# The first weight tile split in halves between token blocks, and later blocks transposed inside the projection, in layer one of an encoder kernel

## The chip, the cores and the metric

The kernel runs on one core of one Trainium2 chip. The metric is the device time of one execution of the whole program in microseconds (us). All arithmetic is on 32-bit values. The engines are named as in the profile: PE is TensorE (PEld its weight loads), DVE is VectorE, ACT is ScalarE, POOL is GpSimd, SP is SyncE. SP here issues nearly all DMA transfers.

## The reference

Two request batches of 256 tokens each run through two layers of an encoder with a model width of 1024. What matters here is how each layer begins:

```
h = rms_norm(x, ln_mix[l])        # 512 tokens x 1024
z = h @ w_in[l]                   # 1024 x 3488, split into
# [c_q 384 | c_kv 256 | k_rope 32 | q_B 512 | k_B 128 | v_B 128 | g_A 1024 | g_B 1024]
x = x + (sigmoid(g_A) * (MLA(c_q, c_kv, k_rope) @ W_oA)
         + sigmoid(g_B) * (WinGQA(q_B, k_B, v_B) @ W_oB)) @ W_out
x = x + HierMoE(rms_norm(x, ln_ffn[l]))   # top group, then top-2 of 8 experts in it
```

After the second layer comes a last `rms_norm`.

## The kernel before

The two batches are treated as one list of 512 tokens, cut into four token blocks of 128 (`C = 4`, index `c`), with tokens on the partitions. Every engine has one instruction stream, written out by hand in program order, and the streams meet at semaphores (`wait_ge` and `then_inc`). There is no scheduler: an engine does its instructions strictly in the order of the code. The loop over the two layers `l` is unrolled.

**Split arithmetic.** Each projection is done as three matmuls (`mm3`, L1158): an operand is cut into a high part (a rounded copy) and a low part (the rest), and the products low x high, high x low and high x high are added up in one bank of PSUM. High parts are made by ACT (a Copy), low parts by DVE (a subtraction). For weights these are `high_part` (L621) and `low_part` (L848).

**The first normalisation.** For each block `c`, ACT squares and sums the 1024 values and takes the root (`norm_root`, L626). DVE takes the reciprocal and scales the block (`norm_chunk`, L828), which raises `h_ready`. PE transposes the block in eight 128x128 pieces, four to a bank (`norm_transposes`, L1164). ACT copies the two banks to `hT_in_high` (L653), and DVE writes `hT_in_low` (`norm_low`, L841). Both are then ready for PE as the moving or the fixed operand.

**The projection.** `w_in` is loaded in five parts. Part 0 holds the columns c_kv, k_rope and v_B, 416 columns for each of 8 slices of 128 rows: 3328 values per partition, called `in_parts[0]`, or the first weight tile. It comes by two DMAs (L403, L404). PE loops over 13 output tiles `t`. The tiles 0 to 3 are the four token blocks times part 0, each 8 slices `k` of three 128x416 matmuls, so 24 matmuls. The tiles 4 to 7 use part 1 (128x384), the tiles 8 to 12 the other parts (128x512).

**Order in layer one, before.** ACT: root of block 0, root of block 1, the high part of all of part 0 (L649), roots of blocks 2 and 3, then the high copies of all blocks. DVE: scale block 0, scale block 1, the low part of all of part 0 (L866), low part of block 0, scale block 2, low part of block 1, scale block 3, low parts of blocks 2 and 3. PE: transposes of blocks 0 and 1, then tile 0; transposes of block 2, then tile 1; transposes of block 3, then tile 2; then tile 3. PE waits for `w_in0_low` and the block's two `hT_in_low` before tile 0. In layer two, part 0 is split on POOL instead (L527 to L529), far ahead.

**What follows.** After the last token block, ACT makes the high part of part 1 and DVE its low part, for tile 4. A small matmul at the start of tile 3 gives a bias table, which goes through DVE (L874) and a DMA of POOL (L539). ACT waits for that DMA before it splits parts 2 and 3 (L673 to L675). The attention stage, the output projection, the router and the expert stage follow. Their DMAs wait for counts that PE raises (`dense_used`).

Of the kernel before, what the change touches and what calls it, by code (L numbers as in the profile page):

```python
# [10 lines left out]
ALU = mybir.AluOpType  # L11
ACT = mybir.ActivationFunctionType
AX = mybir.AxisListType

P = 128
# [4 lines left out]
C = T // P  # L20
KD = D // P
# [31 lines left out]
N_KV = N_TOK - D_CQ  # L53
# [38 lines left out]
def encoder_kernel(nc, x_prompt, x_sample, rel_bias, w_in, ln_cq, ln_ckv, w_uq, w_ukv, w_oa,  # L92
# [3 lines left out]
    with ctx:  # L96
# [255 lines left out]
        N_PARAM = 7  # L352

        IN_ORDER = {1: 0, 4: 1, 2: 2, 3: 3}
        LAST_UNITS = (0, 2, 1, 3, 4, 5, 6, 7)

        def chunk_split(j):
# [154 lines left out]
        def _(pool):  # L512
# [6 lines left out]
            for l in range(L):  # L519

                if l > 0:
                    w = in_parts[0]
                    pool.wait_ge(xs_ps, pool.snap(passes_before) * (2 * PAIRS))
                    pool.nop(nofuse=True)
                    pool.wait_ge(in_in[0], l * 32 + 32)
                    pool.nop(nofuse=True)
                    pool.tensor_copy(w.flat_high, w.flat).then_inc(w_in0_high, 1)  # L527
                    pool.wait_ge(w_in0_high, l + 1)
                    pool.tensor_tensor(w.flat_low, w.flat, w.flat_high, ALU.subtract).then_inc(w_in0_low, 1)  # L529
                    pool.drain()  # L530
                pool.wait_ge(layer_done, pool.snap(passes_before) * C + C)
# [85 lines left out]
        def _(act):  # L617
# [14 lines left out]
            def norm_copy(ns, c):  # L632
# [2 lines left out]
                act.wait_ge(hT_ps, ns * 8 + 2 * c + 1)  # L635
                act.activation(hT[:, 0:4, tok], ps, ACT.Copy).then_inc(hT_act, 1)

            act.dma_start(gain, gains[0:1, :].broadcast_to([P, D])).then_inc(gain_in, 16)
            act.wait_ge(const_in, 16)
            act.activation(spare, eps, ACT.Sqrt)  # L640
            for l in range(L):

                for c in range(C):
                    act.wait_ge(x_in[c], 16)
                    act.wait_ge(layer_done, act.snap(passes_before) * C + c + 1)
                    norm_root(c)
                    if l == 0 and c == 1:
                        act.wait_ge(in_in[0], 32)
                        act.activation(in_parts[0].flat_high, in_parts[0].flat, ACT.Copy).then_inc(w_in0_high, 1)  # L649
                for c in range(C):  # L650
                    for i in (2 * c, 2 * c + 1):
                        act.wait_ge(hT_ps, l * 16 + i + 1)
                        act.activation(hT_in[0][:, 4 * (i % 2):4 * (i % 2) + 4, c * P:(c + 1) * P],  # L653
                                       bank[i % 4][:, :].rearrange("p (k t) -> p k t", k=4), ACT.Copy).then_inc(hT_in_high, 1)
                high_part(in_parts[1], in_in[1], l * 16 + 16)

                for t in range(0, NZ, 2):
# [165 lines left out]
        def _(dve):  # L823
# [36 lines left out]
            for l in range(L):  # L860
                dve.wait_ge(gain_in, l * 32 + 16)
                for c in range(C):
                    norm_chunk(l * 2, c)
                    if l == 0 and c == 1:
                        dve.wait_ge(w_in0_high, 1)
                        dve.tensor_tensor(in_parts[0].flat_low, in_parts[0].flat, in_parts[0].flat_high, ALU.subtract).then_inc(w_in0_low, 1)  # L866
                    if c >= 1:
                        norm_low(l, c - 1)
                norm_low(l, C - 1)
                low_part(l, 0, in_parts[1])  # L870
# [278 lines left out]
        def _(pe):  # L1149
# [27 lines left out]
            pe.wait_ge(const_in, 16)  # L1177
            for l in range(L):
                norm_transposes(l * 2, 0)
                norm_transposes(l * 2, 1)  # L1180

                for t in range(NZ):
                    if t >= 4:
                        pe.wait_ge((z_act, z_dve)[t % 2], l * NZ_OUT + t // 2 - 1)
                    if t < 4:
                        if 1 <= t < 3:
                            norm_transposes(l * 2, t + 1)
                        if t == 0:
                            pe.wait_ge(w_in0_low, l + 1)
                        pe.wait_ge(hT_in_low, l * 8 + 2 * t + 2)  # L1190
                    if t == 3 and l == 0:
                        pe.wait_ge(const_bias, 48)
                        mm(bank[0][0:H, :], makings[0:BUCKETS, 0:H], makings[0:BUCKETS, 512:1024], True, True).then_inc(bias_ps, 1)
                    part = 0 if t < 4 else 1 if t < 8 else 2 if t < 10 else 3 if t < NZ_K else 4
                    if t in (4, 8, 10, NZ_K):
                        pe.wait_ge(w_low, l * SPLITS + IN_ORDER[part] + 1)
                    b = z_bank(t)
                    for k in range(KD):
                        if t < 8:
                            w = in_parts[part]  # L1200
                            tok = slice(t % 4 * P, (t % 4 + 1) * P)
                            m = mm3(b[:, 0:PARTS[part][1]], [h[:, k, tok] for h in hT_in], (w.high[:, k, :], w.low[:, k, :]), k == 0, k == KD - 1)
                        else:
                            w = in_parts[part] if t < NZ_K else k_part
                            col = slice(t % 2 * P, (t % 2 + 1) * P)
                            m = mm3(b[:, :], (w.high[:, k, col], w.low[:, k, col]), [h[:, k, :] for h in hT_in], k == 0, k == KD - 1)
                    m.then_inc(z_ps, 1)
                    if t in (3, 7, 9, 11, NZ - 1):
                        pe.drain().then_inc(dense_used, 1)
# [301 lines left out]
```

## Time and profile before

| | us |
|---|---|
| median of 3 runs | 1386.55 |
| lowest and highest | 1379.80, 1386.73 |
| the profiled execution, its own time | 1388.14 |
| its span, from the first to the last instruction | 1386.3 |
| busy in it: PE, DVE, ACT, POOL | 1248.8, 551.3, 414.5, 215.7 |
| start of the first 128x416 matmul in it | 23.14 |

The profiled execution is 1.59 us above the median of the three timed runs. 1.84 us of it lie outside the span. Times in the rows below are counted from the start of the span. A busy time of an engine in parallel with another is no cost by itself: what sets the end is the chain of waits.

### The profile page before, as it was taken

How to read it: one execution, taken by the hardware profiler on the slowest of the kernel's cores; microseconds unless marked ns; L12 is line 12 of the kernel's file. 1: busy time of each engine (PE TensorE's matmuls, PEld its weight loads, DVE VectorE, ACT ScalarE, POOL GpSimd, SP SyncE). 2: the span in 40 equal slices, each digit the busy share in tenths (PEclk: the TensorE clock that was granted, in tenths of full speed). 3: DMA queues.
4: the chain of work that ended last, by engine and by line, in shares of the span. 5: the costliest groups of instructions: out<-in, count | busy, mean ns of one | idle time of the engine just before them, and what ended most of it. 6: DMA issues, size and time to landing. Idle time of an engine off the chain costs nothing.

```text
span 1386.3 us, 15934 instructions
## 1 busy us (share of the span) xinstructions
PE 1248.8 (90%) x5822; PEld 818.4 (59%) x5822; DVE 551.3 (40%) x848; ACT 414.5 (30%) x809; POOL 215.7 (16%) x214
## 2 busy tenths in 40 slices
PE   4998879999975999999899898899999579999997
PEld 4975557777763444444388655577778434444443
DVE  3345552344242233333464455434342513333335
ACT  3425662222121212222251356422231112212223
POOL 1333540000002111110204325200000031111000
PEclk9999999999995999999999999999999779999999
DMA  9503003332056999999903120043310869999991
GB/s 279 171 16 91 1 1 107 91 91 76 31 206 266 396 415 416 416 414 417 344 2 125 28 64 1 2 150 92 91 62 16 328 257 415 415 416 416 417 412 78
DMA packets 119448, 278.44 MB, mean 201 GB/s; under 512 B 12976, under 2 KB 74928, under 8 KB 102992
## 3 DMA queue, kind: packets, MB, share of 16 engines
q1 hardware_dynamic: 111680, 259.00, 49.4%
q0 software_dynamic: 6400, 13.74, 3.0%
q10 hardware_dynamic: 1296, 4.72, 0.9%
q8 instruction: 47, 0.77, 0.2%
q14 instruction: 25, 0.20, 0.0%
HBM read 279.51 MB, written 8.40 MB: 208 GB/s over the span
## 4 chain that ended last, share of the span: by engine, by line
PE 75%; DMA 10%; DVE 6%; ACT 3%; issue 3%; DVEq 1%; ACTq 1%; SPq 1%; POOL 0%; POOLq 0%
PE bank L1156 70%; DMA arena<-w_up 5%; DMA ring<-w_up 3%; PE bank L1404 2%; PE bank L1277 2%; ACT arena L743 1%; PE bank L1173 1%; DMA x<-x_prompt 1%; DVE arena L833 1%; DVE small L973 1%; DMA arena<-token_rows,idx 1%; ACT arena L747 1%; SPq L472 0%; PE bank L1443 0%; DVE arena L968 0%
## 5 line engine op out<-in xcount | busy, mean ns | idle before, releaser
L1156 PE MATMUL bank<-arena 128*64 128x512 f32 (+5 forms) x1442 | 329.6, 517 | 34.6 <-DVEq L1115 15.0
L1156 PEld LDWEIGHTS bank<-arena 128*64 128x64 f32 (+2 forms) x1442 | 153.2, 156 | 186.3 <-issue 133.5
L1156 PE MATMUL bank<-ring,arena 128*64 128x512 f32 (+1 forms) x800 | 190.6, 607 | 7.0 <-issue 2.5
L1156 PE MATMUL bank<-y_parts,chosen 128*128 128x512 f32 x512 | 135.2, 408 | 5.5 <-DVE y_parts L1139 5.3
L1156 PEld LDWEIGHTS bank<-ring,arena 128*64 128x64 f32 (+1 forms) x800 | 64.5, 142 | 121.5 <-issue 121.5
L608 POOL MEMSET arena<- 128x1024 f32 x32 | 30.7, 959 | 657.7 <-DVEq L1125 448.0
L1094 DVE TENSOR_TENSOR x<-x,bank 128x512 f32<-128x512 f32 x128 | 87.9, 687 | 61.6 <-PE bank L1156 61.6
L1156 PEld LDWEIGHTS bank<-y_parts,chosen 128*128 128x128 f32 x512 | 92.2, 191 | 28.1 <-issue 8.7
L1156 PE MATMUL bank<-hT_gate_low,w_chunk_high 128*128 128x512 f32 x256 | 103.8, 406 | 3.5 <-issue 3.1
L1156 PE MATMUL bank<-hT_gate_high,w_chunk_low 128*128 128x512 f32 x256 | 102.0, 399 | 0.0
L1156 PE MATMUL bank<-hT_gate_high,w_chunk_high 128*128 128x512 f32 x256 | 101.8, 398 | 0.0
L1130 DVE TENSOR_TENSOR arena<-arena,bank 128x256 f32<-128x256 f32 x32 | 13.5, 421 | 220.1 <-ACT arena L801 220.1
L579 POOL TENSOR_TENSOR arena<-arena,small 128x1024 f32<-128x1024 f32 x32 | 61.3, 1917 | 135.3 <-DVE small L957 135.3
L814 ACT ACTIVATE y_parts<-bank,small 128x512 fp32r<-128x512 f32 x64 | 44.0, 688 | 127.8 <-PE bank L1156 127.8
L851 DVE TENSOR_TENSOR w_chunk_low<-ring,w_chunk_high 128x3072 fp32r<-128x3072 f32 x14 | 47.0, 3359 | 85.3 <-ACT w_chunk_high L624 85.3
L1139 DVE SCALAR_TENSOR_TENSOR y_parts<-bank,small,y_parts 128x512 fp32r<-128x512 f32 x64 | 47.9, 750 | 78.7 <-ACT y_parts L814 78.7
L801 ACT ACTIVATE arena<-bank 128x256 f32<-128x256 f32 x32 | 12.3, 385 | 209.3 <-PE bank L1156 209.3
L624 ACT ACTIVATE w_chunk_high<-ring 128x3072 fp32r<-128x3072 f32 x14 | 38.8, 2772 | 88.9 <-DMA ring<-w_in 88.7
L1156 PEld LDWEIGHTS bank<-hT_gate_low,w_chunk_high 128*128 128x128 f32 x256 | 48.7, 190 | 21.2 <-issue 10.1
L1404 PE MATMUL bank<-cst,arena 128*128 128x128 f32 x256 | 41.6, 289 | 16.1 <-DMA arena<-token_rows,idx 16.1
L1156 PEld LDWEIGHTS bank<-hT_gate_high,w_chunk_high 128*128 128x128 f32 x256 | 48.6, 190 | 12.0
L1156 PEld LDWEIGHTS bank<-hT_gate_high,w_chunk_low 128*128 128x128 f32 x256 | 48.7, 190 | 11.0
(209 smaller groups left out, 1846.0 us busy)
## 6 DMA issues: line engine op xcount, KB each, us to landing
ring<-w_gate SPq DMA_DIRECT2D x32, 1024.0 KB, 14.5
ring<-w_up SPq DMA_DIRECT2D x32, 1024.0 KB, 18.8
ring<-w_down SPq DMA_DIRECT2D x32, 1024.0 KB, 18.9
arena<-w_gate SPq DMA_DIRECT2D x32, 1024.0 KB, 15.9
arena<-w_up SPq DMA_DIRECT2D x32, 1024.0 KB, 20.1
arena<-w_down SPq DMA_DIRECT2D x32, 1024.0 KB, 19.7
ring<-w_in SPq DMA_DIRECT2D x36, 512.0 KB, 6.6
ring<-w_in SPq DMA_DIRECT2D x4, 1024.0 KB, 12.7
```

What stands on the lines that cost most here:

```text
L579: pool.tensor_tensor(p_, p_, rowinv[:, n % 2, :].unsqueeze(2).broadcast_to([P, C, S]), ALU.mult).then_inc(prob_ready, 1)
L608: pool.memset(xrows[:, r % 4, :], 0.0)
L624: act.activation(part.flat_high, part.flat, ACT.Copy).then_inc(w_high, 1)
L743: e = act.activation(soft[:, n % 2, c, :], soft[:, n % 2, c, :], ACT.Exp, bias=negmax[:, n % 2, c:c + 1], scale=1.0, accum_out=rowsum[:, n ...
L747: e = act.activation(soft[:, n % 2, c, 0:S], bank[2 * (n % 2) + i][:, b * S:(b + 1) * S], ACT.Exp, bias=negmax[:, n % 2, c:c + 1], scale=M ...
L814: act.activation(y_parts[r // 2 % 2][:, 0, n, half * 512:(half + 1) * 512], bank[4 + half][:, :], ACT.Copy, scale=w_slot[:, r:r + 1]).then ...
L851: dve.tensor_tensor(part.flat_low, part.flat, part.flat_high, ALU.subtract).then_inc(w_low, 1)
L1094: dve.tensor_tensor(part, part, bank[6 + n % 2][:, :], ALU.add).then_inc(combine_done, 1)
L1139: dve.scalar_tensor_tensor(out=y[:, 1, n, cols], in0=bank[4 + half][:, :], scalar=w_slot[:, r:r + 1], in1=y[:, 0, n, cols], op0=ALU.mult, ...
L1156: return pe.matmul(out, lhsT, rhs, start=first, stop=last)
L1277: m = pe.transpose(bank[4 + b][:, (k * 2 + i) * P:(k * 2 + i + 1) * P], soft[:, m_ % 2, 2 * b + i, k * P:(k + 1) * P], ident)
L1404: m = pe.transpose(bank[u][:, k * P:(k + 1) * P], xrows[:, r % 4, at:at + P], ident)
```

## The change

The change touches layer one only (`l == 0`), apart from a counter that starts one higher in layer two because the high and the low part of the first weight tile are now made in two steps.

- ACT takes the root of block 0, makes the two halves of the high part of the first weight tile (1664 values per partition each), copies the transposed block 0, and only then takes the roots of blocks 1, 2 and 3.
- DVE scales block 0, makes the two halves of the low part, makes the low part of block 0, and only then scales block 1.
- PE transposes block 0 and goes to tile 0. The transposes of block `t + 1` are done inside tile `t`, after its first two slices (`k == 2`, so after six matmuls), for `t` of 0, 1 and 2.

```diff
+        IN0_HALVES = slice(0, 4 * (N_KV + P)), slice(4 * (N_KV + P), KD * (N_KV + P))
...
-                    pool.wait_ge(w_in0_high, l + 1)
+                    pool.wait_ge(w_in0_high, l + 2)
...
+            def norm_high(l, c):
+
+                for i in (2 * c, 2 * c + 1):
+                    act.wait_ge(hT_ps, l * 16 + i + 1)
+                    act.activation(hT_in[0][:, 4 * (i % 2):4 * (i % 2) + 4, c * P:(c + 1) * P],
+                                   bank[i % 4][:, :].rearrange("p (k t) -> p k t", k=4), ACT.Copy).then_inc(hT_in_high, 1)
...
                     norm_root(c)
-                    if l == 0 and c == 1:
+                    if l == 0 and c == 0:
                         act.wait_ge(in_in[0], 32)
-                        act.activation(in_parts[0].flat_high, in_parts[0].flat, ACT.Copy).then_inc(w_in0_high, 1)
-                for c in range(C):
-                    for i in (2 * c, 2 * c + 1):
-                        act.wait_ge(hT_ps, l * 16 + i + 1)
-                        act.activation(hT_in[0][:, 4 * (i % 2):4 * (i % 2) + 4, c * P:(c + 1) * P],
-                                       bank[i % 4][:, :].rearrange("p (k t) -> p k t", k=4), ACT.Copy).then_inc(hT_in_high, 1)
+                        for half in IN0_HALVES:
+                            act.activation(in_parts[0].flat_high[:, half], in_parts[0].flat[:, half], ACT.Copy).then_inc(w_in0_high, 1)
+                        norm_high(0, 0)
+                for c in range(int(l == 0), C):
+                    norm_high(l, c)
...
                     norm_chunk(l * 2, c)
-                    if l == 0 and c == 1:
-                        dve.wait_ge(w_in0_high, 1)
-                        dve.tensor_tensor(in_parts[0].flat_low, in_parts[0].flat, in_parts[0].flat_high, ALU.subtract).then_inc(w_in0_low, 1)
-                    if c >= 1:
+                    if l == 0 and c == 0:
+                        for i, half in enumerate(IN0_HALVES):
+                            dve.wait_ge(w_in0_high, i + 1)
+                            dve.tensor_tensor(in_parts[0].flat_low[:, half], in_parts[0].flat[:, half], in_parts[0].flat_high[:, half],
+                                              ALU.subtract).then_inc(w_in0_low, 1)
+                        norm_low(0, 0)
+                    if c >= 1 + int(l == 0):
                         norm_low(l, c - 1)
...
                 norm_transposes(l * 2, 0)
-                norm_transposes(l * 2, 1)
+                if l > 0:
+                    norm_transposes(l * 2, 1)
...
-                        if 1 <= t < 3:
+                        if l > 0 and 1 <= t < 3:
                             norm_transposes(l * 2, t + 1)
                         if t == 0:
-                            pe.wait_ge(w_in0_low, l + 1)
+                            pe.wait_ge(w_in0_low, l + 2)
...
                     for k in range(KD):
+                        if l == 0 and t < 3 and k == 2:
+                            norm_transposes(l * 2, t + 1)
```

On DVE, at the start of layer one, the order before is this (SCALAR_TENSOR_TENSOR is the scaling of a block, 128x3328 the low part of the first weight tile, `hT_in_low` the low part of a block):

```order
L831 RECIPROCAL small<-small 128x1
L833 SCALAR_TENSOR_TENSOR arena<-x,small,lns 128x1024
L831 RECIPROCAL small<-small 128x1
L833 SCALAR_TENSOR_TENSOR arena<-x,small,lns 128x1024
L866 TENSOR_TENSOR w_in_low<-ring,w_in_high 128x3328
L845 TENSOR_TENSOR hT_in_low<-bank,hT_in_high 128x4x128 x2
L831 RECIPROCAL small<-small 128x1
L833 SCALAR_TENSOR_TENSOR arena<-x,small,lns 128x1024
```

The order on DVE in the changed kernel, at the same place:

```order
L838 RECIPROCAL small<-small 128x1
L840 SCALAR_TENSOR_TENSOR arena<-x,small,lns 128x1024
L874 TENSOR_TENSOR w_in_low<-ring,w_in_high 128x1664 x2
L852 TENSOR_TENSOR hT_in_low<-bank,hT_in_high 128x4x128 x2
L838 RECIPROCAL small<-small 128x1
L840 SCALAR_TENSOR_TENSOR arena<-x,small,lns 128x1024
L838 RECIPROCAL small<-small 128x1
L840 SCALAR_TENSOR_TENSOR arena<-x,small,lns 128x1024
```

The low parts of the weight tile and of block 0 have moved ahead of the scaling of block 1.

On PE, at the start of layer one, before (L1173 are the transposes of 128x128, the rest the first matmuls of tile 0):

```order
L1173 MATMUL bank<-cst,arena 128x128 x16
L1156 MATMUL bank<-w_in_low,hT_in_high 128x416
L1156 MATMUL bank<-w_in_high,hT_in_low 128x416
L1156 MATMUL bank<-w_in_high,hT_in_high 128x416
L1156 MATMUL bank<-w_in_low,hT_in_high 128x416
```

And in the changed kernel, where L1183 are the transposes and L1166 the matmuls:

```order
L1183 MATMUL bank<-cst,arena 128x128 x8
L1166 MATMUL bank<-w_in_low,hT_in_high 128x416
L1166 MATMUL bank<-w_in_high,hT_in_low 128x416
L1166 MATMUL bank<-w_in_high,hT_in_high 128x416
L1166 MATMUL bank<-w_in_low,hT_in_high 128x416
L1166 MATMUL bank<-w_in_high,hT_in_low 128x416
L1166 MATMUL bank<-w_in_high,hT_in_high 128x416
L1183 MATMUL bank<-cst,arena 128x128 x8
L1166 MATMUL bank<-w_in_low,hT_in_high 128x416
```

Eight of the first sixteen transposes have moved behind the sixth matmul of tile 0.

On ACT, before (ACTIVATE of 128x1024 and 128x1 are the root of a block, `w_in_high` the high part of the weight tile):

```order
L628 ACTIVATE arena,small<-x 128x1024
L630 ACTIVATE small<-small,cst 128x1
L649 ACTIVATE w_in_high<-ring 128x3328
L645 ISA
L628 ACTIVATE arena,small<-x 128x1024
```

And in the changed kernel:

```order
L629 ACTIVATE arena,small<-x 128x1024
L631 ACTIVATE small<-small,cst 128x1
L658 ACTIVATE w_in_high<-ring 128x1664 x2
L643 ACTIVATE hT_in_high<-bank 128x4x128 x2
L653 ISA
L629 ACTIVATE arena,small<-x 128x1024
```

The root ahead of the weight tile is that of block 1 before and that of block 0 now, and the copies of block 0 follow the weight tile at once.

## Rows read from the trace of the kernel before

**Rows 1.** The page's chain that ended last, shares of the span by engine.

```profile
PE 75%; DMA 10%; DVE 6%; ACT 3%; issue 3%; DVEq 1%; ACTq 1%; SPq 1%; POOL 0%; POOLq 0%
```

**Rows 2.** Chain of waits, 0 to 62 us: start us, us, what (xcount).

```profile
2.93 10.71 DMA x<-x_prompt
...
13.75 1.06 ACT arena L628
...
15.15 2.99 ACTq L629
...
18.17 3.62 DVE w_in_low L866
21.79 0.60 DVE hT_in_low L845
...
23.14 6.26 PE bank L1156 x24
29.40 0.87 PE bank L1173 x8
30.27 4.54 PE bank L1156 x24
```

**Rows 3.** The second DMA of the first weight tile: ns; first and last start us.

```profile
L404 SPq DMA_DIRECT2D ring<-w_in x1: 708/708/708, 2.2 to 2.2; - x1
...
DMA to landing us min/median/max: 10.2/10.2/10.2
```

**Rows 4.** Timeline of ACT, 0 to 130 us: start us, us, what (idle before).

```profile
18.04 1.04 ACT L628 ACTIVATE arena<-x 128x1024 f32<-128x1024 f32 x1
...
20.85 2.04 ACT L653 ACTIVATE hT_in_high<-bank 128x512 fp32r<-128x512 f32 x4
```

**Rows 5.** ACT groups by form, 0 to 60 us: xcount, busy us, mean ns, idle.

```profile
L649 ACT ACTIVATE w_in_high<-ring 128x3328 fp32r<-128x3328 f32 x1 | 3.0, 2963 | 0.0
...
L624 ACT ACTIVATE w_k_high<-ring 128x1024 fp32r<-128x1024 f32 x1 | 1.1, 1079 | 0.0
```

**Rows 6.** DVE groups by form, 0 to 60 us.

```profile
L833 DVE SCALAR_TENSOR_TENSOR arena<-x,small,lns 128x1024 f32<-128x1024 f32 x4 | 5.1, 1284 | 0.3
...
L851 DVE TENSOR_TENSOR w_k_low<-ring,w_k_high 128x1024 fp32r<-128x1024 f32 x1 | 1.2, 1203 | 0.0
```

**Rows 7.** Timeline of PE, 10 to 24 us: the first three matmuls of tile 0.

```profile
23.14 0.68 PE L1156 MATMUL bank<-w_in_low,hT_in_high 128*128 128x416 f32 x1 [4.30 <-DVE hT_in_low L845]
23.62 0.55 PE L1156 MATMUL bank<-w_in_high,hT_in_low 128*128 128x416 f32 x1
23.97 0.55 PE L1156 MATMUL bank<-w_in_high,hT_in_high 128*128 128x416 f32 x1
```

**Rows 8.** Timeline of all engines, 39 to 46.5 us, where part 1 is due.

```profile
39.06 3.36 DVE L851 TENSOR_TENSOR w_in_low<-ring,w_in_high 128x3072 fp32r<-128x3072 f32 x1 [1.86 <-ACT w_in_high L624]
...
46.16 0.41 PE L1156 MATMUL bank<-w_in_low,hT_in_high 128*128 128x384 f32 x1 [0.26 <-issue]
```

**Rows 9.** Waits of PE, 100 to 210 us: us in total, times, longest us.

```profile
PE bank L1156 <- ACTq L718: 4.9, 3, 2.2
PE bank L1277 <- POOL arena L579: 3.8, 2, 2.5
PE bank L1156 <- ACT arena L706: 3.2, 2, 1.7
```

**Rows 10.** Timeline of PE in the attention stage of layer one, two sets of transposes.

```profile
111.63 1.91 PE L1277 MATMUL bank<-cst,arena 128*128 128x128 f32 x8 [2.10 <-ACT arena L695]
...
118.54 1.04 PE L1277 MATMUL bank<-cst,arena 128*128 128x128 f32 x8
```

**Rows 11.** Busy us by stretch: PE, PEld, DVE, ACT, POOL, granted clock, DMA share, GB/s.

```profile
20.00:25.00 5.00, 1.86 (x5) 1.82 (x6) 4.92 (x7) 2.82 (x7) 0.00 (x0) 1.00 1.10 351
...
110.00:115.00 5.00, 3.37 (x12) 3.05 (x13) 0.15 (x1) 2.64 (x5) 1.90 (x1) 0.67 0.77 220
...
200.00:220.00 20.00, 15.93 (x84) 11.83 (x85) 8.70 (x11) 8.96 (x19) 4.15 (x2) 0.91 0.07 21
```

## The prediction, made before the changed kernel was run

> **What bounds the kernel now.** I read the page's chain first: three quarters of the span that set the end are PE's own work [rows 1]. So a change pays here only if it lets PE start earlier, takes instructions from it, or closes a gap in it. The change removes no matmul and no byte. What is left is the time before PE's first real matmul, and I read the chain of waits at the start for it. There the reader is to see a staircase [rows 2]: the DMA of token block 1 lands at 13.64 (2.93 + 10.71), ACT takes that block's root, ACT makes the high part of the whole first weight tile, DVE makes the low part, then the low part of block 0, and PE starts tile 0 at 23.14. From there PE runs without a gap to speak of: 24 matmuls, 8 transposes, 24 matmuls, and so on. None of the first three steps is needed by tile 0 in this order: the weight tile is held up behind block 1's root on ACT, and block 1 landed later than the weight tile did. The weight tile's second DMA was issued at 2.2 and took 10.2 us, so it lay there at 12.4 [rows 3]; ACT began on it at 15.15.
>
> **The change, part by part.**
>
> Start of the weight split. ACT's wait is now for 12.4 instead of for block 1. It begins about 0.1 us after a landing (13.64 to 13.75 in [rows 2]), so at 12.5. ACT has been idle until then, since block 0's root is long done.
>
> High halves. 3328 values cost 2963 ns and 1024 values 1079 ns [rows 5], so 0.818 ns for each further value; a half of 1664 costs 1079 + 640 x 0.818 = 1602 ns. An ACT instruction starts about 0.1 before the end of the one ahead (15.15 + 2.99 against 18.04 in [rows 2, 4]). First half 12.5 to 14.1, second 14.0 to 15.6. The two copies of block 0 follow, four cost 2.04 [rows 4], so they end at about 16.6. The transposes that they read are long done: they need block 0 alone, which is first in every stream.
>
> Low halves. 3.62 us for 3328 values [rows 2] and 1203 ns for 1024 [rows 6]: 1.05 ns per value, a half costs 1203 + 640 x 1.05 = 1875 ns. DVE begins at 14.15 and ends the first half at 16.0, and the second at 17.8, DVE now being the longer of the two and ACT ahead of it. The split in halves buys the overlap: one piece of 2963 ns and then one of 3.62 us take 6.6 us, the halves 17.8 - 12.5 = 5.3.
>
> PE's start. Before, 21.79 is the end of the weight tile's low part, and PE starts 1.35 later, at 23.14, after two low parts of block 0 [rows 2]. The same step now gives 17.8 + 1.35 = 19.15. PE starts tile 0 by 23.14 - 19.15 = 4.0 us earlier. Of this some 2.7 come from the order and 1.3 from the halves.
>
> The transposes of block 1. Before, they stood in PE's wait and cost nothing; now they are in PE's stream. A set of 8 costs 0.87 in the chain [rows 2], at full clock. The sets of blocks 2 and 3 stood in the stream already, between tiles, and move inside them at the same price. Net: 4.0 - 0.87 = 3.1 us.
>
> Is what they wait for there? DVE scales block 1 only after 19.0: a reciprocal of 0.2 and 1.28 [rows 6] give 20.6. ACT has its root by then: copies end at 16.6 and two roots take 20.85 - 18.04 [rows 4], one 1.4, so 18.0, and those of blocks 2 and 3 are done at 19.4 and 20.8. PE comes to block 1 after six matmuls, 0.35 apart in this stretch [rows 7], at 19.15 + 2.2 = 21.4. Nothing is waited for, by 0.8. The price if that cover goes: were these matmuls at full clock, 4.54 / 24 = 0.19 apart [rows 2], PE would come at 20.3 and wait 0.3. Tile 1 wants block 1's low part. Transposes end near 23, ACT and DVE need 1.3 us behind them, and tile 0 still has 18 matmuls, 3.4 us: hidden. Tiles 2 and 3 have 18 matmuls of cover in the same way, where before they had 24, and the two late steps on ACT and DVE fit in either.
>
> What is next late. ACT starts the high part of weight part 1 only after the copies of block 3, whose transposes now stand 6 matmuls (1.1 us) further into tile 2. The step moves by 3.1 - 1.1 = 2.0 us and PE by 3.1. Its low part ended at 39.06 + 3.36 = 42.4 with the first 128x384 matmul at 46.16 [rows 8]: 3.7 us of slack become 2.6. The bias table, for whose DMA ACT waits before it splits parts 2 and 3, goes through DVE behind that low part and so comes some 2 us earlier; parts 2 and 3 are used by tiles 8 to 11 only, with four tiles of part 1 ahead of them. The transfers after that wait for counts of PE and move with it. POOL's wait in layer two has another number and the same event. I take these at nothing, and at most 0.3 us if I misjudge one.
>
> The sum: 1388.14 (the profiled execution, span 1386.3 and 1.84 around it) - 3.1 = 1385.0. That execution was 1.6 above the median of the runs shown; against the median it is 1386.55 - 3.1 = 1383.4. It is 0.22% of the time.
>
> **The term I can't read: the clock.** The stretch 20 to 25 shows a granted clock of 1.00 [rows 11], but the matmuls in it start 0.35 apart [rows 7] and in tile 1 0.19 [rows 2]: PE began at the 1.2 GHz level and went to 2.4 GHz about 3 us into tile 0. Tile 0 took 6.26 where tile 1 took 4.54 [rows 2], so the slow start costs 1.7 us. After the change PE does half as many transposes ahead and then has one unbroken run. If the rise comes as long after the start as before, nothing changes and 3.1 stands. If it stays at the same moment, near 26.2, then 4.0 more us run at half speed: 4.0 x 0.19 / 0.35 = 2.2 of work, less 0.87, and the gain is 1.3. If there is no slow stretch at all, the gain is 3.1 + 1.7 = 4.8. I take 3.1, since in the trace PE had also stood idle for 4.3 us before tile 0 and rose 3 us after.
>
> The Trainium skill ("TensorE: Matmul & The Clock Gate", Part 1) says that the monitor's window runs freely and isn't reset when a kernel starts, so the moment of the rise depends on how the first matmul falls in it. By that rule the rise is tied neither to the start nor to one moment, and the gain would lie anywhere between the 1.3 and the 4.8. The trace, with one start in it, doesn't tell.
>
> **The rivals.**
>
> The rise stays where it was. For it: the idle stretch before tile 0, 4.30 us [rows 7], grows, since the second set of transposes no longer stands ahead of it. Against: the rise came 3 us into the first unbroken run, as if started by it. 1386.55 - 1.3 = 1385.3.
>
> Clock drops further on fall away. The granted clock is 0.67 over 110 to 115 us, after PE waited 2.10 us for ACT; the transposes there took 1.91, and a later set 1.04 [rows 10, 11]. Such a stretch costs (1 - 0.67) x 5 = 1.65 us. Not every wait of this length has one: between 100 and 210 us there are seven others, of up to 2.5 us [rows 9], and the clock fell once more, 0.91 over 200 to 220 [rows 11]. So it hangs on timing, which a shift by 3 us alters. Two fewer, or one and an early rise at the start: 1386.55 - 3.1 - 3.3 = 1380.1. The lowest run before, 1379.80, shows that such times occur.
>
> The same mechanism the other way, and this is the case that ends slower: the waits of the attention stages, in both layers, meet the clock worse. Place: PE behind ACT L718, L706 and POOL L579. Price: 1.65 us a drop. It decides from the second additional drop (3.3 against 3.1), and with three it is +5.0 - 3.1 = +1.9: 1388.4. For it: at least six waits there drew none yet. Against: nothing in the change favours this side, and it needs three of them.
>
> The change doesn't do what it says: the start isn't freed, because the weight tile isn't the late input. If ACT got it only with block 1 at 13.64, all would move by 1.2 and the gain would be 1.9, 1384.6; if also the scaling of block 1 were late inside tile 0, where PE would stand, near 1386. Against: the landing in [rows 3] is 1.2 ahead of block 1's.
>
> **How the numbers follow.** Forecast 0.62 (1383.4, alone 1381.5 to 1385); rise stays 0.12 (1385.3); fewer drops 0.14 (1380.1); more drops 0.08 (1388.4); not freed 0.04 (1386). A measurement of this kernel can tell about 0.5%, 6.9 us, from no change, so faster by that means 1379.6 or less. Half and a little more of the fewer-drops case, makes 0.10, since a time below 1380 turned up before the change too. Slower by that is over 1393.5, which needs six drops: 0.03. The rest, 0.87, is within. The range reaches from the fewer-drops case, 1379, to the more-drops case, 1388.
>
> **What would show it.** In the profile after: the ACT instruction of 128x1664 starts near 12.5 and the last low half ends near 17.8; the first 128x416 matmul starts near 19.2; block 1's transposes begin near 21.4 with no wait for DVE; tile 1's first matmul 3 us earlier than 30.27; the first 128x384 matmul near 43.1, with no wait for the low part of part 1; and the same 3 us at every later landmark up to the attention stage. The spacing of the first matmuls shows the rise. The forecast is wrong if PE waits inside tile 0, if the 3 us are there at 43 and gone by the end with no clock drop to account for them, or if the first low half waits for its high half longer than 0.1.

## The result, and the profile after

| | before | changed |
|---|---|---|
| median of 18 runs each, us | 1385.31 | 1376.68 |
| lowest and highest | 1374.79, 1389.43 | 1371.73, 1382.52 |
| profiled execution, own time | 1388.14 | 1372.49 |

The ratio of the comparison is 0.995, with a 95% interval of 0.9932 to 0.9969: faster, by 4 to 9 us (the two medians alone give 0.9938, the two means 7.1 ± 2.6 us). The forecast was 1383.4, in a range of 1379 to 1388, so the median came out below the range. The two profiled executions lie 15.6 us apart, more than the medians do.

**The start is as the prediction had it.** The chain of waits of the changed kernel, 0 to 120 us (start us, us, what), answers to [rows 2]:

```profile
2.17 10.07 DMA ring<-w_in
12.27 1.60 ACT w_in_high L658
13.89 3.69 DVE w_in_low L874 x2
17.59 0.60 DVE hT_in_low L852
...
18.93 2.42 PE bank L1166 x6
21.35 1.50 PE bank L1183 x8
22.86 4.55 PE bank L1166 x24
27.41 0.87 PE bank L1183 x8
```

The staircase now begins with the weight tile's own DMA instead of token block 1's. The first 128x416 matmul stands at 18.93 instead of 23.14, 4.2 us earlier. PE goes from its sixth matmul to block 1's transposes without a wait. The next landmark [rows 8] moved by 3.13 us:

```profile
43.03 0.41 PE L1166 MATMUL bank<-w_in_low,hT_in_high 128*128 128x384 f32 x1 [0.26 <-issue]
```

The low part of part 1 ended at 37.05 + 3.36 = 40.4, with 2.6 us of slack, as the prediction had it:

```profile
37.05 3.36 DVE L858 TENSOR_TENSOR w_in_low<-ring,w_in_high 128x3072 fp32r<-128x3072 f32 x1 [1.86 <-ACT w_in_high L625]
```

**Where the rest comes from.** SP's issues of DMAs come in the same order in both kernels and make good landmarks: the start of such an issue says how far the program has come. Before less changed, in the first pair of traces (us from the start of the span):

| landmark | before | changed | difference |
|---|---|---|---|
| layer one, w_uq | 46.02 | 42.90 | 3.12 |
| w_oa, the first chunk | 109.77 | 106.64 | 3.13 |
| w_out, end of attention | 217.25 | 211.23 | 6.02 |
| layer two, w_in | 672.46 | 666.49 | 5.97 |
| w_uq | 728.48 | 715.61 | 12.87 |
| w_out | 899.57 | 883.79 | 15.78 |
| y_prompt | 1379.05 | 1363.43 | 15.62 |

3.1 us come from the start, 2.9 from the attention stage of layer one, 6.9 from the first steps of layer two, 2.9 from its attention stage. The change has edited no instruction in any of the last three.

The largest piece first. These are DVE and POOL of the kernel before in layer two (start us, us, what): POOL's subtraction for the first weight tile, and the last of 32 instructions of DVE that build `chosen`.

```profile
683.70 7.22 POOL L529 TENSOR_TENSOR w_in_low<-ring,w_in_high 128x3328 fp32r<-128x3328 f32 x1
683.98 7.48 DVE L1133 TENSOR_TENSOR chosen<-cst,small 128x512 fp32r<-128x512 f32 x1
```

And in the changed kernel:

```profile
678.01 0.68 DVE L1143 TENSOR_TENSOR chosen<-cst,small 128x512 fp32r<-128x512 f32 x1
678.11 7.81 POOL L530 TENSOR_TENSOR w_in_low<-ring,w_in_high 128x3328 fp32r<-128x3328 f32 x1
```

Both instructions read two operands from SBUF, the on-chip memory. The one that starts second waits for the first: with POOL 0.28 us ahead, DVE took 7.48 us instead of 0.68; with DVE 0.10 us ahead, POOL took 7.81 instead of 7.22. The Trainium skill ("SBUF — State Buffer", section "Who interferes with whom") says just this: a DVE instruction with two SBUF inputs contends with a GpSimd instruction that reads SBUF, and issue order decides who blocks. The trace agrees, and it was to be read before the run: the waits of PE in the kernel before (us in total, times, longest) had a row for it.

```profile
PE bank L1156 <- DVE y_parts L1139: 5.3, 1, 5.3
```

The changed kernel has no such row. PE also came out of this wait at the slower of its two levels: the granted clock is 0.50 from 692 to 695.

The attention stage. A drop here is a stretch in which the granted clock falls. It is the third figure from the end of a row. The first stretch of the kernel before is 110 to 115 in [rows 11], at 0.67; this is one near the end of the stage:

```profile
205.00:210.00 5.00, 3.01 (x12) 2.72 (x13) 3.08 (x3) 2.78 (x6) 1.93 (x1) 0.73 0.02 5
```

And of the changed kernel at the same two places:

```profile
107.00:112.00 5.00, 3.48 (x18) 2.84 (x19) 0.66 (x3) 2.55 (x5) 1.89 (x1) 1.00 0.76 198
195.00:200.00 5.00, 3.56 (x16) 1.66 (x16) 4.92 (x8) 3.19 (x12) 2.02 (x2) 0.66 0.00 0
```

The drop behind the wait for ACT L695 is gone; that wait itself is the same, 2.1 us in both. The second drop comes some 5 us earlier in the stage. There PE is slow while POOL is still busy with the softmax, and the next wait shrinks from 2.50 us for POOL [rows 9] to 1.29:

```profile
202.59 1.06 PE L1290 MATMUL bank<-cst,arena 128*128 128x128 f32 x8 [1.29 <-ACTq L725]
```

In this pair the drop in one place cost more than the drop in the other. What each is worth follows below, from all the traces.

### The profile page after: what moved, and what is told of

Read it like the earlier page. It is cut to its first block, busy times and chain, and to the rows that moved or that the text cites. A ratio compares the mean times of both kernels' runs of the same rounds, so it can differ in the third digit from the quotient of the medians.

```text
span 1370.7 us, 15936 instructions
## 1 busy us (share of the span) xinstructions
PE 1243.4 (91%) x5822; PEld 813.1 (59%) x5822; DVE 545.1 (40%) x849; ACT 414.5 (30%) x810; POOL 216.0 (16%) x214
## 4 chain that ended last, share of the span: by engine, by line
PE 76%; DMA 10%; DVE 5%; ACT 4%; issue 2%; DVEq 1%; ACTq 1%; SPq 1%; POOLq 0%
PE bank L1166 71%; DMA arena<-w_up 5%; DMA ring<-w_up 3%; PE bank L1417 2%; PE bank L1290 2%; ACT arena L750 1%; PE bank L1183 1%; ACT arena L754 1%; DMA ring<-w_in 1%; DVE small L983 1%; DMA arena<-token_rows,idx 1%; DVE arena L840 1%; SPq L473 0%; DVE arena L978 0%; PE bank L1456 0%
## 5 line engine op out<-in xcount | busy, mean ns | idle before, releaser
L1166 PE MATMUL bank<-arena 128*64 128x512 f32 (+5 forms) x1442 | 331.0, 521 | 34.4 <-DVEq L1125 15.0
L1166 PEld LDWEIGHTS bank<-arena 128*64 128x64 f32 (+2 forms) x1442 | 153.1, 157 | 186.9 <-issue 135.6
L1166 PE MATMUL bank<-ring,arena 128*64 128x512 f32 (+1 forms) x800 | 190.7, 608 | 6.9 <-issue 2.5
L1166 PEld LDWEIGHTS bank<-ring,arena 128*64 128x64 f32 (+1 forms) x800 | 64.5, 142 | 121.5 <-issue 121.5
L1166 PE MATMUL bank<-y_parts,chosen 128*128 128x512 f32 x512 | 133.9, 404 | 0.3
L1166 PE MATMUL bank<-hT_gate_low,w_chunk_high 128*128 128x512 f32 x256 | 102.6, 401 | 3.6 <-issue 3.2
L1166 PEld LDWEIGHTS bank<-y_parts,chosen 128*128 128x128 f32 x512 | 91.1, 188 | 22.7 <-issue 3.3
L1166 PE MATMUL bank<-hT_gate_high,w_chunk_low 128*128 128x512 f32 x256 | 101.1, 395 | 0.0
L1166 PE MATMUL bank<-hT_gate_high,w_chunk_high 128*128 128x512 f32 x256 | 101.1, 395 | 0.0
L1166 PEld LDWEIGHTS bank<-hT_gate_low,w_chunk_high 128*128 128x128 f32 x256 | 48.0, 187 | 21.1 <-issue 10.2
L1166 PEld LDWEIGHTS bank<-hT_gate_high,w_chunk_high 128*128 128x128 f32 x256 | 48.0, 187 | 11.7
L1166 PEld LDWEIGHTS bank<-hT_gate_high,w_chunk_low 128*128 128x128 f32 x256 | 48.0, 188 | 10.9
```

The lines of the kernel that those rows point to most:

```text
L1166: return pe.matmul(out, lhsT, rhs, start=first, stop=last)
```

## The experiments

Twelve runs were made, of eight kernels, in three sets. A ± is a 95% interval from the scatter of single runs. In each trace I read three things: the start of the first 128x384 matmul (the start of the program), the time from the issue of w_oa to that of w_out in layer one (attention), and from w_in to w_uq in layer two (the meeting of POOL and DVE).

### Both kernels again, unchanged

> The kernel before, unchanged, once more, for its trace and five more times. In the first trace of it POOL's subtraction for the first weight tile of layer two began 0.28 us ahead of DVE's last building of 'chosen', and that DVE instruction took 7.48 us instead of 0.68, with PE waiting 5.3 us behind it. In the trace of the changed kernel DVE began 0.10 us ahead, and its instruction took 0.68. Theory A (a lottery of that meeting, drawn by when the weight DMA lands, with the change having nothing to do with it): this kernel shows both outcomes, times near 1375 without the meeting and near 1385 with it. Theory B (the change shifts the two against each other): this kernel nearly always has the meeting, and the changed one seldom. Theory C (clock drops further on make the difference): times go with the number of drops, whatever DVE's instruction took.

> The changed kernel, unchanged, once more. Theory A: both outcomes as often as in the kernel before, times near 1372 and near 1380. Theory B: mostly the fast outcome. Theory C: as the clock has it. All theories: the first 128x416 matmul near 18.9 us and the first 128x384 matmul near 43.0 us, since the start of the program is the same each time.

Measured: the kernel before 1379.23 (12 runs, 1373.89 to 1386.23), the changed one 1381.4 (12 runs, 1372.20 to 1385.92), and 30 more runs of the kernel before 1383.6. Against those 30 the changed kernel stands at 0.9982, interval 0.9956 to 1.0009: no difference that this set can tell. The outcomes of the meeting were swapped. The kernel before, this time with DVE ahead:

```profile
681.26 0.92 DVE L1133 TENSOR_TENSOR chosen<-cst,small 128x512 fp32r<-128x512 f32 x1
681.72 7.67 POOL L529 TENSOR_TENSOR w_in_low<-ring,w_in_high 128x3328 fp32r<-128x3328 f32 x1
```

The changed kernel, this time with POOL ahead:

```profile
676.76 7.21 POOL L530 TENSOR_TENSOR w_in_low<-ring,w_in_high 128x3328 fp32r<-128x3328 f32 x1
677.07 7.46 DVE L1143 TENSOR_TENSOR chosen<-cst,small 128x512 fp32r<-128x512 f32 x1
```

Its PE waited 5.3 us for y_parts, just as the kernel before had in its first trace. From w_in to w_uq it took 57.8 us, against 56.0 in the kernel before with the meeting and 49.1 to 49.4 in either without it. Theory B (the change shifts the two against each other) has lost in the form in which it was put: each kernel shows each outcome. DVE's instruction starts 11.52 or 11.53 us after SP issues w_in in all four traces. POOL's subtraction starts 11.22 to 11.99 after it, because POOL's copy ahead of it waits for that DMA: the copy starts 8.17 to 8.94 after the issue and takes 2.96 each time. The draw is in the landing. Four traces can't exclude that the change shifts the odds a little, but they show no path by which it would.

The 0.92 in the kernel before, instead of 0.68, is the same thing with POOL's copy. DVE started 0.37 us before the end of that copy (678.67 + 2.96), and ended 0.55 after it. One warmed trace has it too (0.90). In the two long cases DVE ended 0.54 and 0.56 after POOL's subtraction.

### The meeting taken away, in both kernels

The edit is the same in either kernel (here the kernel before):

```diff
                     pool.wait_ge(w_in0_high, l + 1)
+                    pool.wait_ge(pick_ready, pool.snap(passes_before) * PAIRS)
+                    pool.nop(nofuse=True)
                     pool.tensor_tensor(w.flat_low, w.flat, w.flat_high, ALU.subtract).then_inc(w_in0_low, 1)
```

> The kernel before, but in layer two POOL's subtraction for the first weight tile waits until DVE's last 'chosen' is built (one more wait for pick_ready). Same arithmetic. Theories A and B: DVE's last 'chosen' takes 0.68 in every run, POOL's subtraction ends near 692 and is not needed before PE's tile 0 of layer two at about 700, and the time falls from 1385 to 1377 to 1379, with the upper group of times gone. Theory C: no change of the median, 1385.

> The changed kernel with the same additional wait on POOL in layer two. Theories A and B: the two outcomes fall together at the lower one, about 1373 to 1375, and it stands 3.1 us (0.22%) below the kernel before with the same wait, which would be the worth of the change at the start. Theory C: 1376 to 1377 as without the wait, and the distance to the other one stays at 7 to 8 us.

> The kernel before with the additional wait on POOL in layer two, unchanged from the earlier run, for a second trace and more times. In the first set its times fell into two groups, 1375.4 to 1376.3 and 1379.2 to 1381.2. Theory A (what is left is a set of further draws, clock drops and meetings of POOL with DVE in the attention stages, the same for both kernels): two groups again, mean near 1378. Theory B (the change still shifts these): the same here, but the changed kernel with the wait stays in one group. The first 128x416 matmul near 23.1, the first 128x384 between 46.2 and 47.4, since the time at which PE's clock rises varies by about 1 us.

> The changed kernel with the additional wait, unchanged from the earlier run. Theory A: its times also show an upper group, about 4 us above 1372 to 1373, the mean lies near 1374.5, and over both sets the distance to the kernel before with the same wait comes to 3.1 to 3.6. Theory B: one group near 1372.5 again, and the distance stays near 5 us.

Measured: the kernel before with the wait 1377.73 (12 runs) and 1376.38 (6 runs), the changed one with it 1372.88 (7) and 1374.92 (6). Against the kernel before without it the ratios were 0.997 (0.995 to 0.999), 0.9937 (0.9913 to 0.996), 0.9926 (0.9901 to 0.9952) and 0.9926 (0.9906 to 0.9947). DVE's instruction, in the kernel before with the wait, is short, and POOL comes behind it:

```profile
681.62 0.68 DVE L1135 TENSOR_TENSOR chosen<-cst,small 128x512 fp32r<-128x512 f32 x1
682.46 7.36 POOL L531 TENSOR_TENSOR w_in_low<-ring,w_in_high 128x3328 fp32r<-128x3328 f32 x1 [1.35 <-DVE chosen L1135]
```

It is so in all four traces with the wait, and from w_in to w_uq they take 48.4 to 49.1 us. The spread of single runs fell from 4.1 us (standard deviation, kernel before) to 2.2 in the first set. By means over all runs, the wait takes 5.2 ± 1.3 us off the kernel before (105 runs of it, from all comparisons together, against 18) and 4.3 ± 2.0 off the changed one (30 against 13). The upper group that stayed in the first set of the kernel before (1379.2 to 1381.2) is not explained by the meeting. In the second set one of six runs lies up there (1382.66), and one of six of the changed kernel at 1379.49. The landmarks show one more thing that varies: from w_out of layer two to y_prompt lie 479.1 to 480.2 us in ten of all fourteen traces and 481.8 to 482.5 in four, two of each kernel. The difference gathers over the passes of the expert stage. Its cause was not looked for.

The distance between the two kernels with the wait is 4.9 ± 1.6 us in the first set, 2.1 ± 3.0 in the second and 3.7 ± 1.6 over both. Theory C (drops alone) has lost too: it expected no change of the medians.

### The halves, and the place of the transposes

Both in the changed kernel with the additional wait. Without halves:

```diff
-        IN0_HALVES = slice(0, 4 * (N_KV + P)), slice(4 * (N_KV + P), KD * (N_KV + P))
+        IN0_HALVES = (slice(0, KD * (N_KV + P)),)
```

with the counts of the two waits lowered by one.

> The changed kernel with the additional wait, but the first weight tile of layer one split in one piece on ACT and one on DVE instead of halves; the order of the work is that of the change. By the terms of the prediction: first 128x416 matmul at 18.9 + 1.3 = 20.2, first 128x384 at 43.0 + 1.3 = 44.3 give or take 0.4 for the rise of the clock, median 1.3 us above the kernel with halves. A rival, that the halves cost as much in fixed time as they overlap: first 128x416 matmul at 18.9 to 19.2.

The first 128x416 matmul started at 20.24, 1.3 later than the 18.93 to 19.01 with halves: that term was right. The first 128x384 came at 45.47, 2.3 later, of which the rise of the clock has 1.0 (24 matmuls after block 1's transposes took 5.47 us, where 4.55 is full clock). The times can't tell 1.3 us from nothing: the median is 1374.42 (6 runs) against 1372.88 and 1374.92.

The transposes between the tiles:

```diff
-                        if l == 0 and t < 3 and k == 2:
-                            norm_transposes(l * 2, t + 1)
...
+                        if l == 0 and t > 0:
+                            norm_transposes(l * 2, t)
```

> The changed kernel with the additional wait, but the transposes of blocks 1, 2 and 3 stand ahead of tiles 1, 2 and 3 instead of inside the tile before. Same first 128x416 matmul, 18.9. Now each tile needs the high copy and the low part of the block just transposed. From rows of the changed kernel: 1.6 us lie between the start of a set's transposes and the last low part beyond what the transposes themselves take, so PE waits about 1.3 to 1.6 us at each of tiles 1, 2 and 3, and the first 128x384 matmul comes at 47 to 48 instead of 43. Rival: the wait is hidden by PE's queue, and it comes at 43 to 44.

The waits of PE from 18 to 50 us, in this kernel:

```profile
PE bank L1168 <- DVE hT_in_low L854: 10.8, 4, 6.0
```

Of these, 6.0 is the wait ahead of tile 0, and 4.8 in three waits are new, 1.6 each, as expected. The first 128x384 matmul came at 50.44, beyond the 47 to 48 expected. It is not part 1 that held it: its low part was done at 48.0, and PE stood idle for 0.26 us ahead of that matmul, as in every other trace. PE fell to the slower level inside tile 3. Two matmuls of that tile and its last one:

```profile
44.32 0.55 PE L1168 MATMUL bank<-w_in_high,hT_in_high 128*128 128x416 f32 x1
44.67 0.55 PE L1168 MATMUL bank<-w_in_low,hT_in_high 128*128 128x416 f32 x1
...
49.83 0.35 PE L1168 MATMUL bank<-w_in_high,hT_in_high 128*128 128x416 f32 x1
```

From 44.3 to 47.4 the matmuls start 0.35 apart instead of 0.19, and the granted clock is 0.57 over 44 to 48. That is some 1.6 us. With the 4.8 of the waits it leaves 0.7 of the 7.1 us to the kernel with the transposes inside, for a later rise at the start and the restarts after the waits. This is one trace. The drop came behind three waits that the other kernels don't have, and none of the other thirteen traces shows one before 100 us.

The median was 1380.68 (8 runs), 0.9969 of the kernel before (0.994 to 0.9998), and the mean lies 6.7 ± 1.9 us above that of the same kernel with the transposes inside. The change stands on this edit: what it adds to PE's stream must be where 18 matmuls hide the copies behind it.

### The rise of the clock taken out, in both kernels

These have dummy transposes of a constant in PE's idle time ahead of tile 0 (the kernel before: 22, 34 and 42; the changed one: 22 and 54), and the additional wait on POOL:

```diff
+            def warm(n):
+                for _ in range(n):
+                    pe.transpose(bank[7][:, 0:P], ident, ident)
...
             pe.wait_ge(const_in, 16)
+            warm(22)
             for l in range(L):
                 norm_transposes(l * 2, 0)
+                if l == 0:
+                    warm(54)
```

> The kernel before with the additional wait on POOL, and with dummy transposes of a constant (22, 34 and 42, into a bank not yet used) in PE's idle stretches ahead of tile 0 of layer one, so that PE's clock has risen before tile 0. They add work that the reference doesn't need and end before PE's inputs come. Theory D (what the change gained beyond the 3.1 us is the moment of the clock's rise, which moves with PE's start and by which later drops fall on waits or on work): first 128x416 matmul at 23.1 as before, its matmuls 0.19 apart at once, the first 128x384 at 44.5 to 45.0 in every trace instead of 46.0 to 47.4, so 1.7 us or more off the median of 1376.4. Theory A (all of it chance, clock drops as often in both): the same at the start.

> The changed kernel with the additional wait on POOL and dummy transposes (22 and 54) ahead of tile 0. First 128x416 matmul at 18.9 to 19.0, 0.19 apart; PE comes to block 1's transposes at 20.1, where DVE has them ready at 20.2; the first 128x384 matmul at 41.6 to 42.0 in every trace instead of 42.7 to 43.3. Theory D: with the rise out of the way in both kernels, the later clock drops fall alike, and the distance to the other warmed kernel is 3.0 us on the median. Theory A: 3.0 us as well in expectation, but the attention stage of layer one, 104.4 us from the first load of w_oa to that of w_out in all four traces of the changed kernel so far against 105.6 to 107.5 before, was then chance, and takes 104.4 to 107.5 in both. If the change had some other lasting effect on that stage, it would stay at 104.4 here and at 106 to 107 in the other.

> The same kernel as the warmed one before, once more, for a second trace: the first 128x384 matmul within 0.3 us of the first trace's, and the attention stage of layer one by theory D and A as above.

> The same kernel as the warmed changed one, once more, for a second trace: the first 128x384 matmul within 0.3 us of the first trace's, and the attention stage of layer one by theory D and A as above.

| traces | first 128x384 | attention of layer one |
|---|---|---|
| kernel before, 4 (two with the wait) | 46.16, 46.50, 47.36, 46.01 | 107.5, 106.2, 105.6, 107.3 |
| changed, 4 (two with the wait) | 43.03, 42.74, 43.31, 43.21 | 104.6, 104.5, 104.3, 104.3 |
| kernel before, warmed, 2 | 44.53, 44.60 | 105.8, 107.4 |
| changed, warmed, 2 | 41.60, 41.57 | 107.3, 106.2 |

Tile 0 of the kernel before, warmed, now takes 4.76 us instead of 6.26 [rows 2]:

```profile
23.02 4.76 PE bank L1158 x24
```

The first 128x384 in the warmed kernels agrees to 0.07 us within each kernel, where the others vary by 1.4 and 0.6, and the two lie 3.0 us apart: about the 4.0 of the earlier start less the set of transposes. The medians were 1375.61 (12 runs) and 1375.07 (8) against 1373.28 (10) and 1371.02 (7), and by means over both sets the distance is 3.3 ± 1.5 us. The dummies take 2.3 ± 1.3 us off the mean of the kernel before and 1.9 ± 1.8 off that of the changed one.

The attention stage of the changed kernel is no longer the shorter one. Its length goes with the clock in all fourteen traces. A first drop comes behind PE's wait for ACT L695 or doesn't: the granted clock over the 6 us after the issue of w_oa is 0.72 or 1.00, behind the same wait of 2.1 us. A second one comes 88 to 95 us after that issue (early) or 95 to 102 (late), at a granted clock of 0.76 over those 7 us.

| first drop | second drop | traces | attention of layer one |
|---|---|---|---|
| yes | late | kernel before: the first, the second with the wait, the second warmed; changed: transposes between, the first warmed | 107.3 to 107.5 |
| yes | early | kernel before: again; changed: without halves, the second warmed | 106.2 |
| no | late | kernel before: the first with the wait, the first warmed | 105.6, 105.8 |
| no | early | changed: the first, again, both with the wait | 104.3 to 104.6 |

So the first drop costs about 1.7 us and the later place of the second about 1.2. The change does nothing lasting to the stage: four traces of kernels with it, or with a variant of it, have the first drop, and in layer two the same stage takes 104.3 to 104.5 us in eight traces, three of them of kernels without it. Theory D isn't borne out as it was put: with the rise taken out the drops still differ between two traces of one kernel (105.8 and 107.4). That all four unwarmed traces of the changed kernel with its transposes and halves in place had the short form may come from its earlier start, or it is chance. The runs can't settle that.

## Why the prediction was wrong, and what of it was right

**PE's start.** Right: 18.93 to 19.01, forecast 19.15; ACT's halves from 12.27, forecast 12.5; low parts done near 17.6, forecast 17.8. One reading in it is off: it says that tile 0 needs none of the first three steps of the staircase. The third, ACT's high part of the weight tile, it does need. Only block 1's landing and root stood in its way, and the sum was made so.

**The transposes inside the projection.** Right: 0.87 each at full clock, no wait for block 1, and tiles 0 to 2 hide what follows. The set of block 1 took 1.50 in the first trace, since it began at the slower level.

**What is next late.** Right: 2.6 us of slack left at part 1, and the landmark at 43.0.

**The worth of the change.** 3.1 us was forecast. At w_uq it was 3.12 in the first pair of traces, 2.98 with the rise of the clock out of the way, and in time 3.7 ± 1.6 and 3.3 ± 1.5 in the two pairs of kernels freed of the meeting. Over all runs of the two original kernels, 105 and 30, it is 4.6 ± 1.8.

**The rise of the clock.** The forecast let it come as long after the start as before. The traces show that it doesn't come at a fixed distance: between the first 128x416 and the first 128x384 matmul lie 22.99 to 24.26 us in the kernel before. The Trainium skill's rule that the prediction cites (the monitor's window runs freely) agrees with that. In the mean it is worth little: the first 128x384 lies 3.4 us earlier in the changed kernel (means of four traces each) where it is 3.0 with the rise out of the way.

**The step that failed** is the one in "What is next late": "The transfers after that wait for counts of PE and move with it. POOL's wait in layer two has another number and the same event. I take these at nothing, and at most 0.3 us if I misjudge one." What POOL does behind that wait is no fixed term. Its start hangs on a DMA's landing, which came at times 0.8 us apart after the same issue, and on it hangs whether DVE's `chosen` takes 0.68 us or 7.48, and the stretch from w_in to w_uq 49.1 to 49.4 us or 56.0 to 57.8. A term of 6.6 to 8.7 us that is drawn anew in each execution stood at nothing. The rivals named another mechanism, the clock, at 1.65 us a drop (measured: about 1.7 for the first one of the attention stage), so the range ended at 1379, and in the first pair of traces the drops gave 5.8 us beside the 6.9 of the meeting.

The numbers follow from it. The median of the unchanged kernel lay at 1385.31, 1383.60, 1379.23, 1385.86 and 1384.22 in five sets, that of the changed one at 1376.68 and 1381.40. Of the 9.9 us between the 1386.55 from which the forecast was reckoned and the 1376.68 measured, 1.2 are the base, whose three runs gave a median above that of 18, 3.1 are the change, and 5.5 stand beyond it. With the line drawn 3.1 us lower for the changed kernel (1376 against 1379.1), 10 of 18 runs of it and 16 of 18 of the kernel before lay above in the first comparison, 9 of 12 and 28 of 42 in the second, whose ratio was 0.9982. So the 5.5 us are read as mostly another draw of the meeting and of the clock. This is inferred: single runs without a trace don't show their draw. The runs show no hand of the change in it, and they don't exclude a small one. By that reading it was bad luck that the first median fell below the range, and good luck that the second, 1381.40, falls inside it. Neither of them tests the 3.1 us. The landmarks and the kernels freed of the meeting do.

The row of a 5.3 us wait for y_parts, and a longest instance of 7480 ns for `chosen` where the median is 684, were in the profile before and were not followed. They would have given a two-peaked forecast.

**Better than both.** The changed kernel with POOL's one additional wait has a mean of 1374.0 over 13 runs (changed alone 1378.3 over 30), and with the dummy transposes 1372.1 over 17. Against the kernel before the last was 0.993 (0.9905 to 0.9955) and 0.9915 (0.9887 to 0.9944).

## What to carry to other kernels

Read the longest instance of each group as well as its mean: one instruction in 32 that took eleven times as long as its fellows marked a race of two engines here, and its outcome changed from run to run with no edit at all. Before a gain of a few tenths of a per cent is put down to an edit, compare landmarks in several traces of both kernels, and take the switch away in both. Work added to an engine's stream is cheap only where enough of its own work stands between it and the one who needs the result.

## What the runs showed of the hardware

- POOL and DVE, each with two operands in SBUF, excluded each other for the whole instruction: a start 0.28 us too late cost DVE 6.8 us, one 0.10 us too late cost POOL 0.6. DVE's instruction ended 0.54 to 0.56 us after POOL's. POOL's copy of the same tile, with one operand, held it too (0.92 instead of 0.68).
- DVE's instructions with an operand in PSUM were not held by the same POOL instruction: four additions to x in the 7.8 us beside it took 0.7 each, as always.
- A drop of PE's granted clock came behind the same wait of 2.1 us in eight of fourteen traces and not in six. It cost about 1.7 us there. A second drop cost about 1.2 us less where it came some 5 us earlier in the stage; in the pair compared above, the wait for POOL behind it was then shorter (1.29 us against 2.50).
- The slow start of PE lasted 3.3 us after its first projection matmul in one trace of the kernel before, and 6.0 in another, where tile 0 took 7.50 us instead of 6.26. Dummy transposes of a constant in the idle time ahead of it took it away, and delayed nothing.
